# Sixteen value heads of a gated delta rule: keys and queries left unnormalised, their lengths carried as numbers per token

## The reference

```
qkv = silu(causal_short_conv(concat([gq, gk, gv]), conv_w))
cq, ck, cv = split(qkv)
q = cq * rsqrt(sum(cq * cq) + EPS) * 128 ** -0.5        # l2norm per token and head
k = ck * rsqrt(sum(ck * ck) + EPS)
A = strict_lower((k * beta) @ k.T * L)                  # L: decays between tokens
T = inverse(I + A)
u = T @ (v * beta);  w = T @ (k * beta * exp(gamma))
qk = lower(q @ k.T * L)
v_new = u - w @ S;  o = (q * exp(gamma)) @ S + qk @ v_new
o = o * rsqrt(mean(o * o) + EPS) * out_norm * silu(gz)  # rmsnorm per token and value head
```

## Time and profile before

| what | value |
|---|---|
| time, median of 3 runs | 1371.02 us (1370.97 to 1371.08) |
| span of the profiled execution | 1369.8 us, 1.2 us under that median |
| PE busy | 1355.6 us, 99% |
| DVE busy | 1045.3 us, 76% |
| ACT busy | 801.3 us, 58% |
| one call of `head` in the loop | 50.1 us |
| PE's granted clock, 40 slices | 9 tenths or more in each |

### The profile page before, as it was taken

How to read it: one execution, slowest core, us unless ns; L and a number is a source line. 1 busy time by engine, 2 the same in 40 slices (tenths; PEclk the granted TensorE clock), 3 DMA queues, 4 the chain that set the end, 5 groups by cost and what they waited for, 6 DMA issues and landing times.

```text
span 1369.8 us, 24310 instructions
## 1 busy us (share of the span) xinstructions
PE 1355.6 (99%) x8592; PEld 1211.1 (88%) x8592; DVE 1045.3 (76%) x1622; ACT 801.3 (58%) x1310; POOL 23.3 (2%) x71
## 2 busy tenths in 40 slices
PE   8999999999999999999999999999999999999998
PEld 8888888989888888888899999999999998988886
DVE  5798888777666686666778888888888877666665
ACT  4445554644443364444668898898898853544444
POOL 6000000000000000000000000000000000000000
PEclk9999999999999999999999999999999999999999
DMA  8565554655556746666574453554543286666661
GB/s 265 153 193 155 150 147 153 201 196 190 184 191 197 226 137 202 184 184 186 153 199 117 131 154 99 146 144 112 141 130 122 82 213 203 173 207 197 187 184 62
DMA packets 291214, 227.80 MB, mean 166 GB/s; under 512 B 10882, under 2 KB 270164, under 8 KB 291156
## 3 DMA queue, kind: packets, MB, share of 16 engines
q1 hardware_dynamic: 291012, 226.75, 55.6%
q10 hardware_dynamic: 144, 0.26, 0.1%
HBM read 225.90 MB, written 1.08 MB: 166 GB/s over the span
## 4 chain that ended last, share of the span: by engine, by line
PE 93%; DVE 3%; ACT 1%; DVEq 1%; issue 1%; DMA 1%; ACTq 0%; SPq 0%
PE M L2066 10%; PE G L2066 9%; PE M L2054 7%; PE M L2055 7%; PE M L2056 7%; PE G L2049 5%; PE M L2068 5%; PE G L2051 5%; PE G L2050 5%; PE G L2068 5%; PE G L2188 2%; PE G L2940 2%; PE M L2749 1%; PE M L2767 1%; PE G L2054 1%; PE G L2056 1%
## 5 line engine op out<-in xcount | busy, mean ns | idle before, releaser
L1203 DVE TENSOR_TENSOR w_lo<-w_raw,w_hi 128x2048 fp32r<-128x2048 f32 (+2 forms) x249 | 481.3, 1936 | 132.4 <-ACT w_hi L647 128.1
L647 ACT ACTIVATE w_hi<-w_raw 128x2048 fp32r<-128x2048 f32 x198 | 377.9, 1909 | 169.4 <-PE M L2068 54.3
L2049 PE MATMUL G<-xa,w_hi 128*128 128x256 f32 x592 | 176.8, 299 | 0.0
L2051 PE MATMUL G<-xa,w_lo 128*128 128x256 f32 x592 | 167.2, 282 | 0.0
L2050 PE MATMUL G<-xa,w_hi 128*128 128x256 f32 x592 | 167.0, 282 | 0.0
L2066 PE MATMUL M<-xa,w_hi 128*128 128x512 f32 x600 | 151.5, 394 | 0.0
L2066 PE MATMUL G<-xa,w_hi 128*128 128x512 f32 x568 | 142.5, 393 | 0.0
L2066 PEld LDWEIGHTS M<-xa,w_hi 128*128 128x128 f32 x600 | 107.8, 189 | 19.8
L2066 PEld LDWEIGHTS G<-xa,w_hi 128*128 128x128 f32 x568 | 104.0, 188 | 21.3 <-issue 1.2
L2054 PE MATMUL M<-w_hi,xb 128*128 128x512 f32 x300 | 117.3, 391 | 0.0
L2055 PE MATMUL M<-w_lo,xb 128*128 128x512 f32 x300 | 117.1, 390 | 0.0
(11 more groups left out here) (446 smaller groups left out, 2540.6 us busy)
## 6 DMA issues: line engine op xcount, KB each, us to landing
w_raw<-in_w_in SPq DMA_DIRECT2D x150, 512.0 KB, 4.7
w_raw<-in_ffn_w_in SPq DMA_DIRECT2D x88, 512.0 KB, 5.1
w_raw<-in_w_ff SPq DMA_DIRECT2D x64, 512.0 KB, 4.2
w_raw<-in_ffn_w_out SPq DMA_DIRECT2D x44, 512.0 KB, 5.0
w_raw<-in_w_in SPq DMA_DIRECT2D x33, 256.0 KB, 3.2
w_raw<-in_w_out SPq DMA_DIRECT2D x16, 512.0 KB, 4.0
w_raw<-in_w_branch_gdn SPq DMA_DIRECT2D x16, 512.0 KB, 5.3
w_raw<-in_w_branch SPq DMA_DIRECT2D x12, 512.0 KB, 4.2
```

What stands on the lines that cost most here:

```text
L647: nc.scalar.activation(w_hi[:, slot, :], w_raw[:, slot, :], ACT.Copy).then_inc(hi_ready, 1)
L1203: return v.tensor_tensor(dst, src, hi.bitcast(F32), ALU.subtract)
L2049: mm(out_, w[0], x[0], start=first, stop=False)
L2051: return mm(out_, w[1], x[0], start=False, stop=last_)
```

## The change

Query and key stay as they leave the silu. The products key x key and key x query are made of the unnormalised vectors, and the lengths are put back as numbers per token:

- key x key is made first, right behind the silu (`kk_done`). DVE takes its diagonal, which is every token's sum of squares, by a product with the identity and a sum along the row, adds EPS, takes the reciprocal and multiplies beta by it (`key_lengths` on DVE).
- ACT makes the key's length by Ln and Exp of 128 x 2 numbers (`key_lengths` on ACT) and scales the values by it while it copies them (`values_scaled`).
- PE turns the query into bank 3 of `M` (`qt_done`), ACT sums its squares, times EPS, along the rows (`query_lengths`, `q_len_ready`), and DVE adds EPS squared (`q_bias`). The output norm of the next call uses `q_bias` as its eps (`delta_rstd`), one Ln for each block of tokens.
- The ones product, the squares of 128 x 512, their Ln and Exp, the product that normalised query and key, and two small DVE operations (lines 1929 and 1930) are gone.

```diff
+            def delta_rstd():
+                for x in range(4):
+                    nc.scalar.activation(zi[:, x // 2, x % 2, :], M[:, 5, P * x:P * x + P], ACT.Square, accum_out=o_sum[:, x:x + 1])
+                settle()
+                for b in range(TT):
+                    nc.scalar.activation(o_rstd[:, 2 * b:2 * b + 2], o_sum[:, 2 * b:2 * b + 2], ACT.Ln, scale=1.0 / P,
+                                         bias=q_bias[:, b:b + 1])
+                settle()
+                nc.scalar.activation(o_rstd, o_rstd, ACT.Exp, scale=-0.5).then_inc(grs_ready, 1)
+
+            def key_lengths():
+                act.wait_ge(k_len_ready, i + 1)
+                nc.scalar.activation(k_len, k_len2, ACT.Ln)
+                settle()
+                nc.scalar.activation(k_len, k_len, ACT.Exp, scale=0.5)
+                settle()
+
+            def values_scaled():
+                act.wait_ge(vt_done, i + 1)
+                for b in range(TT):
+                    ins = nc.scalar.activation(vsd[:, b, :, :].rearrange("p e c -> p (e c)"), M[:, 0, T * b:T * b + T], ACT.Copy,
+                                               scale=k_len[:, b:b + 1])
+                ins.then_inc(v_ready, 1)
+
+            def query_lengths():
+                act.wait_ge(qt_done, i + 1)
+                for b in range(TT):
+                    ins = nc.scalar.activation(q_sq[:, b, :], M[:, 3, P * b:P * b + P], ACT.Square, scale=RMS_EPS ** 0.5,
+                                               accum_out=q_sum[:, b:b + 1])
+                ins.then_inc(q_len_ready, 1)
...
-                settle()
-                nc.scalar.activation(eg[:, 0:2 * T], acc[:, 0:2, :].rearrange("p n t -> p (n t)"), ACT.Square).then_inc(sq_ready, 1)
...
-            if gemm:
-                act.wait_ge(ss_done, i + 1)
-                nc.scalar.activation(eg[:, 2 * T:4 * T], M[:, 2, :], ACT.Ln, bias=eps[:, 1:2])
-                settle()
-                nc.scalar.activation(eg[:, 2 * T:4 * T], eg[:, 2 * T:4 * T], ACT.Exp, scale=-0.5).then_inc(rs_ready, 1)
...
+            if gemm:
+                key_lengths()
+                values_scaled()
             if main:
                 act.wait_ge(go_done, i)
-                token_rstd(zi.rearrange("p i e c -> p (i e) c"), M[:, 5, :].rearrange("p (x c) -> p x c", c=P), o_sum, o_rstd,
-                           1.0).then_inc(grs_ready, 1)
+                delta_rstd()
             if gemm:
-                act.wait_ge(vt_done, i + 1)
-                nc.scalar.activation(vsd, M[:, 0, :].rearrange("p (i e c) -> p i e c", i=TT, e=2), ACT.Copy).then_inc(v_ready, 1)
+                query_lengths()
...
+            def key_lengths():
+                dve.wait_ge(kk_done, i + 1)
+                v.tensor_tensor(k_sq, kk[:, 0:3:2, :], ident[:].unsqueeze(1).to_broadcast([P, TT, P]), ALU.mult)
+                settle()
+                v.tensor_reduce(k_len2, k_sq, AX_X, ALU.add)
+                settle()
+                v.tensor_scalar(k_len2, k_len2, RMS_EPS, None, ALU.add).then_inc(k_len_ready, 1)
+                settle()
+                v.reciprocal(k_inv2, k_len2)
+                settle()
+                v.tensor_tensor(beta_head.rearrange("p (s i e) -> p s i e", s=2, i=TT),
+                                betas[:, ds(i, 1), :, :, :].rearrange("p h s i e -> p (h s) i e"),
+                                k_inv2.unsqueeze(1).unsqueeze(3).to_broadcast([P, 2, TT, 2]), ALU.mult)
...
             if gemm:
+                key_lengths()
                 v.tensor_copy(yi, ident[:].unsqueeze(1).unsqueeze(1).to_broadcast([P, TT, 2, P]))
             w_low_j(2)
-            if gemm:
-                dve.wait_ge(rs_ready, i + 1)
-                v.tensor_tensor(acc[:, 0:2, :].rearrange("p n t -> p (n t)"), acc[:, 0:2, :].rearrange("p n t -> p (n t)"),
-                                eg[:, 2 * T:4 * T], ALU.mult).then_inc(qn_ready, 1)
...
             if main and gemm:
                 delta_gate(i)
             if gemm:
+                dve.wait_ge(q_len_ready, i + 1)
+                v.tensor_scalar(q_bias, q_sum, RMS_EPS * RMS_EPS, None, ALU.add)
...
             if gemm:
-                pe.wait_ge(sq_ready, i + 1)
-                mm(M[:, 2, :], ones[:], eg[:, 0:2 * T], start=True, stop=True).then_inc(ss_done, 1)
+                pe.wait_ge(silu_ready, i + 1)
+                mm(M[:, 2, 0:T], acc[:, 1, 0:P], acc[:, 1, :], start=True, stop=True)
+                mm(M[:, 2, T:3 * P], acc[:, 1, P:T], acc[:, 1, P:T], start=True, stop=True).then_inc(kk_done, 1)
...
                 pe.wait_ge(vn1_ready, i)
+            if gemm:
+                for b in range(TT):
+                    ins = nc.tensor.transpose(M[:, 3, P * b:P * b + P], acc[:, 0, P * b:P * b + P], ident[:])
+                ins.then_inc(qt_done, 1)
...
             if gemm and not main:
                 pe.wait_ge(gbc_ready, 1)
+                pe.wait_ge(q_len_ready, 1)
...
             if gemm:
-                pe.wait_ge(qn_ready, i + 1)
+                pe.wait_ge(q_len_ready, i + 1)
                 pe.wait_ge(lt_pre, i + 1)
-                for bank, x in ((2, acc[:, 1, :]), (3, acc[:, 0, :])):
-                    mm(M[:, bank, 0:T], acc[:, 1, 0:P], x, start=True, stop=True)
-                    ins = mm(M[:, bank, T:3 * P], acc[:, 1, P:T], x[:, P:T], start=True, stop=True)
-                ins.then_inc(kq_done, 1)
+                mm(M[:, 3, 0:T], acc[:, 1, 0:P], acc[:, 0, :], start=True, stop=True)
+                mm(M[:, 3, T:3 * P], acc[:, 1, P:T], acc[:, 0, P:T], start=True, stop=True).then_inc(qk_done, 1)
```

More of the change, by code:

```diff
@@ L202, in emit @@
     acc = grid(mix(4 * T), n=4, t=T)
-    eg = raw.rearrange("p n t -> p (n t)")[:, 0:4 * T]
+    k_sq, q_sq = (raw[:, n, 4:4 + T].rearrange("p (i c) -> p i c", i=TT) for n in range(2))
     cwt = grid(mix(4 * CONV), j=CONV, n=4)
@@ L217, in emit @@
     h_sum, h_rstd = mix(2), mix(2)
+    k_len2, k_inv2, k_len, q_sum, q_bias = (stat[:, at:at + TT] for at in range(50, 60, TT))
     o_sum, o_rstd = mix(4), mix(4)
@@ L346, in emit @@
                          "tok_ready"))
-    conv_ready, tap_ready, sq_ready, ss_done, rs_ready, vt_done, v_ready, gbc_ready, gam_done, lt_pre, lt_ready = (
-        sem(n) for n in ("conv_ready", "tap_ready", "sq_ready", "ss_done", "rs_ready", "vt_done", "v_ready",
+    conv_ready, tap_ready, silu_ready, kk_done, qt_done, k_len_ready, q_len_ready, vt_done, v_ready, gbc_ready, gam_done, lt_pre, lt_ready = (
+        sem(n) for n in ("conv_ready", "tap_ready", "silu_ready", "kk_done", "qt_done", "k_len_ready", "q_len_ready", "vt_done", "v_ready",
                          "gbc_ready", "gam_done", "lt_pre", "lt_ready"))
-    qn_ready, kq_done, y0_ready, t_done, t_ready, ffn_step = (
-        sem(n) for n in ("qn_ready", "kq_done", "y0_ready", "t_done", "t_ready", "ffn_step"))
+    qk_done, y0_ready, t_done, t_ready, ffn_step = (
+        sem(n) for n in ("qk_done", "y0_ready", "t_done", "t_ready", "ffn_step"))
     zz_done, zc_ready, ww_done, wt_done, xx_ready, yy_ready, yt_done, xc_ready, ntc_ready = (
@@ L1091, in head @@
                 act.wait_ge(conv_ready, i + 1)
-                nc.scalar.activation(acc, acc, ACT.Silu)
+                nc.scalar.activation(acc, acc, ACT.Silu).then_inc(silu_ready, 1)
                 chunk_done(2)
                 nc.scalar.activation(hq, G[:, 1, 0:T], ACT.Silu)
-                settle()
-                nc.scalar.activation(eg[:, 0:2 * T], acc[:, 0:2, :].rearrange("p n t -> p (n t)"), ACT.Square).then_inc(sq_ready, 1)
             log_exp_set()
@@ L1812, in o_low @@
                 low_of(xa_lo[:, k0:k1, :], o_h[:, k0:k1, :], xa_hi[:, k0:k1, :]).then_inc(ohl_ready, 1)
+            kk = M[:, 2, 0:3 * P].rearrange("p (b c) -> p b c", b=3)
+            def key_lengths():
[11 more added lines that the diff above has]
+                                k_inv2.unsqueeze(1).unsqueeze(3).to_broadcast([P, 2, TT, 2]), ALU.mult)
             def gam_copy():
@@ L1952, in head @@
                 settle()
-                dve.wait_ge(kq_done, i + 1)
-                kk = M[:, 2, 0:3 * P].rearrange("p (b c) -> p b c", b=3)
                 for e in range(2):
@@ L1971, in head @@
                 settle()
+                dve.wait_ge(qk_done, i + 1)
                 for e in range(2):
@@ L2865, in head @@
                 pe.wait_ge(vn1_ready, i)
+            if gemm:
+                for b in range(TT):
+                    ins = nc.tensor.transpose(M[:, 3, P * b:P * b + P], acc[:, 0, P * b:P * b + P], ident[:])
+                ins.then_inc(qt_done, 1)
+            if main:
                 for e in range(2):
```

## The result

| kernel | median | ratio to before |
|---|---|---|
| before | 1370.97 us (1370.84 to 1371.18, 7 executions) | |
| changed | 1375.47 us (1374.19 to 1376.12, 7 executions) | 1.0031, 95% interval 1.0022 to 1.0040 |

The account below looks back on a forecast made before the run. It took two chains ending together at inv_z(2), PE's list and an ACT/DVE chain, as the bound. Median 1371.02 + 3.1 (call 0 +2.1, seven looped calls +1.0) = 1374.1 us; range 1371.6 to 1376.7.

Parts of the forecast that it names:

- What bounds the kernel: Looped calls: PE's list and an ACT/DVE chain end together at inv_z(2); cutting PE alone buys nothing.
- The 0.64 taken from PE: PE's list per call: ones product and later key pair go, key x key and two query transposes come; 0.64 less.
- Where PE waits: In the loop, PE idle some 0.7 ahead of inv_z(2), whose load follows DVE's inverse(1) by 0.05.
- the prediction's own sign: Wrong if loop idle time lies elsewhere, above all inv_z(1) or yi's turn, or key x key steps stay equal without call 0's gap.
- all of it lies ahead of `inv_z(2)` and is lost in the wait there: Looped calls: PE's 0.64 saving precedes inv_z(2) and disappears in its wait for DVE's inverse(1).
- ACT's chain: Looped calls, from PE's turned output to grs_ready: steps sum to 3.76, ending 0.13 later than before.
- The loop, +1.0 forecast: DVE's chain and PE's inv_z(2) end 0.14 later per looped call; seven calls +1.0, from 0 to +3.5.
- nothing else in that chain changes: DVE's looped chain: beyond the later gate and q_bias, no further delay; the wait for the products was already over.
- Call 0, +2.1 forecast: Call 0: PE multiplies 2.74 later, awaiting the query's sums; the cheaper later pair returns 0.65; bounds 1.7 to 2.7.
- rival 5: Call 0: PE's clock falls in the 2.5 us pause, half of twice 2.92 us lost, +3, 1377; chance 0.07.
- The sum: Whole kernel: call 0's +2.1 and the loop's +1.0 on the median 1371.02 give 1374.1.

Follow-up runs that it names:

- e4: Changed kernel plus one unused 256-column product of constants (0.43 us) on PE in each looped call; 1375.8 us.
- e5: Changed kernel with e1's bank, the qk_done wait ahead of nt, and ACT's key_lengths and values_scaled ahead of the copy awaiting PE's turned output; 1371.19 us.
- e6: Changed kernel with e1's bank, the qk_done wait ahead of nt, ACT's query squares later and q_bias made one call later; 1370.71 us.
- e9: e5 and e6 combined, DVE's low weights before key_lengths in call 0, plus query transposes behind the previous head's output products; 1367.32 us, ratio 0.9973.
- e11: e5 and e6 combined, call 0's low weights before key_lengths, output products before quarter 15, query transposes behind them, delta_rstd after ACT's second split; 1365.39 us.
- e12: Changed kernel with only DVE's qk_done wait moved, from ahead of the last product of lt to ahead of nt; 1373.88 us.
- e2: Changed kernel with DVE's qk_done wait moved from ahead of line 2008 to ahead of the scan; 1374.15 us.
- e1: Changed kernel with the query turned into bank 5 instead of bank 3 in call 0, so the decays' transposes need not wait; 1372.72 us, ratio 1.0011.
- e3: Changed kernel with three 512-column products of constants on PE during call 0's pause; 1374.24 us, ratio 1.0021.
- e10: The changed kernel unaltered, measured again on the chip of e9 and e11; 1374.29 us, ratio 1.0024.

## Why the prediction held, and where it did not, point by point

- **What bounds the kernel** was read rightly: a chain on ACT and DVE, not PE's list. e4 shows it from one side (0.43 more on PE, 0.02 to 0.03 more in the distance), e5, e6 and e9 from the other (each cut in the chain comes through). The 0.64 taken from PE was real and was lost in waits; e11 gets it back once the chain is short enough.
- **Where PE waits** was wrong, by the prediction's own sign: it called itself wrong if PE's idle time lay at `inv_z(1)` or at the turn of `yi`, and it lies there. It had 0.7 ahead of `inv_z(2)`. The load there does follow the end of `inverse(1)` (880.65 + 0.73 = 881.38) by 0.06, but only 0.14 behind the load ahead of it: PE had already lost 0.49 at the turn of `yi` and 0.42 at `inv_z(1)`. The step that failed is "all of it lies ahead of `inv_z(2)` and is lost in the wait there", and ahead of it the reading that `inv_z(2)` was the tightest wait. In the kernel before, `inv_z(1)` had no room either (its load 0.12 behind the product of `lt`), and the turn of `yi` had 0.25, less than the 0.64 that PE gained. The time is the same, since all three hang on one chain of DVE.
- **ACT's chain**: 3.76 forecast, 3.76 measured, and each step within 0.02 of its term, so this is no luck; the gate 0.05 later, and `q_bias` 0.07 more ahead of the decays (forecast 0.06 and 0.08).
- **The loop, +1.0 forecast.** Measured 0.23 per call on average from call 2 on instead of 0.14, 0.53 in call 1, and about 0.16 in call 7: 1.9 in all. The step that failed is "nothing else in that chain changes". DVE idles 0.10 more ahead of 2008, and in call 1, the first pass of the loop, 0.35 more (0.43 there). The first explanation was the wait that the change moved to this place; e12 took it away from there, and the idle time stayed. In the copy of the code that call 0 runs, the same two operations with the same wait are 0.08 apart. The idle time is absent in e6 to e9 and e11, where `q_bias` has left its place ahead of them, and in e2. That looks like something tied to where instructions stand in DVE's program rather than to what they wait for. The built programs fit it: counted in DVE's instructions from the start, this operation of the loop stands at one and the same place in every kernel that shows the idle time (changed, e1, e3, e4, e5, e12), one place earlier in e6 to e9 and e11, two later in e2 and ten earlier in the kernel before. But no run changed the place alone: the cause stays open.
- **Call 0, +2.1 forecast.** Without the fall of the clock the first distance is 49.23 in e10 and 49.24 in e2, so 2.16 more than 47.07: right in mechanism and size. The chain behind the key product was sized within 0.1 (transposes at 711.52, forecast 711.6, with a start 0.11 earlier).
- **The clock, rival 5,** was given 0.07 and +1.5 to +3. It is not a rival but an addition that comes and goes: of five profiled executions with the idle pause, the granted clock fell in two (changed kernel, e4; 0.3 and 1.1 us after PE had started again) and stayed in three (e2, e10, e12). It costs 50.84 - 49.23 = 1.6 where it falls. The two sets of the changed kernel, 1374.19 to 1376.12 and 1373.65 to 1375.19, fit executions with and without it, and some in between; only the profiled ones say which is which. The prediction's argument took a clock like that of the earlier trace rows for twice its 2.92 us; in fact 3.4 us at the lower level followed. The Trainium skill (TensorE: Matmul & The Clock Gate, Why this matters for your kernels) warns of pauses of more than about 3 us; by these runs one of 2.62 is not safe either.
- **The sum.** 2.16 + 1.9 = 4.1 without the fall, and the medians differ by 3.3 where e10 was measured. The rest lies outside the calls: the last write of the one profiled execution of before ran 0.9 longer behind PE's last product than in any of the others, and the first key product starts 0.1 to 1.0 earlier in the traces of the changed kernels than the ones product in it. That trace is also a longer execution than most: its span is 1369.8, where the executions of before beside e10 have 1369.0 to 1369.8, half of them 1369.2 or less. With one trace of before, that isn't settled. The forecast of 1374.1 is the result of e10 (1374.29); the first set has 1375.47, 1.4 above the forecast and in its range, and the clock's fall, which the forecast left to a rival of 0.07, is in most of its executions by their times. Part of the agreement with e10 is luck: the loop's term was 0.9 short, and 0.8 that no term had went the other way outside the calls.

## What to carry to other kernels

An operation that is taken from the busiest engine buys nothing while another engine's chain ends at the same place: here 0.64 us of PE per call came back only after DVE's and ACT's chain had been shortened by reordering (e5, e6, e9, e11), and then nearly all of it did (50.12 to 49.51). Give the new small operations the idle time that an engine has ahead of its next wait, and a scratch bank of its own to what is read late; the bank and the orders turned 0.3% slower into 0.4% faster with the same arithmetic. And follow a chain through each of its releases, and compare at every one the end of the releasing work with the start of the weight load, and that load with the one ahead of it: `inv_z(1)` was as tight before the change as after it, without any gap in PE's own records, and idle time shows first at the earliest wait that is tight.

## What was unexpected of the hardware

- A pause of 2.62 us on PE, with PE busy all the time before, was followed by some 3.4 us at 1.2 GHz in two of five profiled executions, and by none in three. With three products of constants in the pause the clock read 1.00 (e3), in its one profiled execution; that these held it is suggested by its times and not shown.
- DVE idled 0.18 instead of 0.08 between two neighbouring operations of the loop, whether a wait stood there or not (changed kernel, e12), and 0.43 in the loop's first pass; in call 0's copy of the code, and in the loop with an instruction more or less ahead of them (e2, e6), the same two stood 0.08 to 0.09 apart.
